# The first 60 microseconds by quarters of the channels instead of halves, in a two-block transformer kernel

## The reference

```python
mod = silu(cond) @ w + b                    # ada_w: 1024 x 6144, for the latent and the context condition
shift, scale, gate, ... = split(mod, 6)     # six parts of 1024 channels each
h = x * (1 + scale) + shift                 # on all 512 tokens (latent and context)
z = h @ conv_w_in                           # 1024 x 2560, five parts of 512 columns
a_val, a_gate, b_gate, c_gate, b_val = split(z)
ya = a_val * sigmoid(a_gate)                # then a depthwise convolution of 31 taps, a layer norm ...
```

## Time and profile before

| | |
|---|---|
| median of three runs | 1993.77 us (1989.11 to 1994.6) |
| span of the profiled execution | 1993.6 us |
| TensorE busy | 1775.0 us, 89% |
| VectorE busy | 1016.0 us, 51% |
| ScalarE busy | 418.9 us, 21% |
| GpSimd busy | 559.6 us, 28% |
| bytes moved | 574.31 MB, mean 288 GB/s |
| mean granted clock of TensorE | 0.953 |

### The profile page before, as it was taken

The page is one execution under the profiler, slowest core; times in us unless marked ns, Lnnn a source line. Parts: engine busy times, 40 slices in busy tenths (PEclk is TensorE's granted clock), DMA queues, the critical chain, the costliest instruction groups (busy, mean ns, idle before and its releaser), DMA issues.

```text
span 1993.6 us, 56691 instructions
## 1 busy us (share of the span) xinstructions
PE 1775.0 (89%) x23868; PEld 1227.3 (62%) x23869; DVE 1016.0 (51%) x2422; ACT 418.9 (21%) x838; POOL 559.6 (28%) x423
## 2 busy tenths in 40 slices
PE   7999989999999997999989966666669989999998
PEld 4544456656666664645766744444447767788887
DVE  3798156666676677247255633333347985110001
ACT  2001242211111214115342211111113224110001
POOL 0000026766766772001034523222257000100000
PEclk9999989999999998999989988888889899999999
DMA  9854177999999999514289999999996264433320
GB/s 364 323 207 169 42 264 324 429 428 429 410 430 411 430 428 392 194 46 158 85 330 417 430 429 428 429 428 428 429 409 218 102 234 171 169 127 127 129 104 21
DMA packets 109379, 574.31 MB, mean 288 GB/s; under 512 B 4977, under 2 KB 10225, under 8 KB 84593
## 3 DMA queue, kind: packets, MB, share of 16 engines
q1 hardware_dynamic: 108720, 570.72, 71.3%
q10 hardware_dynamic: 576, 2.43, 0.3%
HBM read 572.08 MB, written 1.05 MB: 287 GB/s over the span
## 4 chain that ended last, share of the span: by engine, by line
PE 64%; DMA 25%; DVE 7%; issue 2%; ACT 2%; SPq 1%; DVEq 0%; ACTq 0%
PE bank L355 25%; DMA ring<-in_expert_w_up 16%; PE bank L569 14%; DMA ring<-in_expert_w_down 8%; PE bank L541 4%; PE bank L999 4%; PE bank L519 3%; PE bank L616 3%; DVE b L1059 2%; PE bank L426 1%; ACT b L1879 1%; PE bank L915 1%; DVE b L1685 1%; DVE h_t L1059 1%; PE bank L718 1%
## 5 line engine op out<-in xcount | busy, mean ns | idle before, releaser
L569 PE MATMUL bank<-ring,b 128*32 128x128 f32 (+1 forms) x13600 | 517.8, 309 | 129.2 <-DMA ring<-in_expert_w_gate 67.1
L569 PEld LDWEIGHTS bank<-ring,b 128*32 128x32 f32 x13600 | 398.9, 115 | 302.5 <-issue 152.6
L1059 DVE TENSOR_TENSOR h_t<-h_t,bank 128x512 f32<-128x512 f32 (+1 forms) x696 | 349.5, 563 | 307.8 <-PE bank L541 307.8
L355 PE MATMUL bank<-h_t,ring 128*128 128x256 f32 (+1 forms) x1600 | 427.0, 429 | 5.9 <-ACT h_t L1879 5.9
L1879 ACT ACTIVATE b<-bank 128x256 f32<-128x256 f32 (+4 forms) x371 | 142.1, 400 | 1267.4 <-PE bank L569 742.3
L355 PEld LDWEIGHTS bank<-h_t,ring 128*128 128x128 f32 x1600 | 308.9, 194 | 117.6 <-issue 78.7
L2308 POOL TENSOR_SCALAR b<-b 128x1024 f32<-128x1024 f32 (+1 forms) x85 | 195.1, 2295 | 58.3 <-POOL b L2316 33.6
L2316 POOL TENSOR_TENSOR b<-b 128x512 f32<-128x512 f32 (+1 forms) x85 | 88.8, 1045 | 404.7 <-PE bank L541 404.7
L541 PE MATMUL bank<-b 32*128 32x512 f32 (+1 forms) x1392 | 171.0, 562 | 8.2 <-DVE h_t L1059 4.7
L1059 DVE TENSOR_TENSOR b<-b,bank 128x128 f32<-128x128 f32 (+3 forms) x124 | 49.9, 406 | 233.4 <-PE bank L355 155.1
L2311 POOL TENSOR_TENSOR b<-b,b 128x1024 f32<-128x1024 f32 (+1 forms) x85 | 161.4, 1899 | 7.1
(11 more groups left out here) (306 smaller groups left out, 1438.0 us busy)
## 6 DMA issues: line engine op xcount, KB each, us to landing
ring<-in_expert_w_gate SPq DMA_DIRECT2D x64, 2048.0 KB, 18.4
ring<-in_expert_w_up SPq DMA_DIRECT2D x64, 2048.0 KB, 20.7
ring<-in_expert_w_down SPq DMA_DIRECT2D x64, 2048.0 KB, 20.9
ring<-in_ada_w SPq DMA_DIRECT2D x24, 2048.0 KB, 14.1
ring<-in_w_mod SPq DMA_DIRECT2D x12, 2048.0 KB, 11.3
ring<-in_w_in SPq DMA_DIRECT2D x6, 2048.0 KB, 10.8
ring<-in_w_ffn_gate SPq DMA_DIRECT2D x5, 2048.0 KB, 8.5
ring<-in_w_ffn_up SPq DMA_DIRECT2D x5, 2048.0 KB, 7.7
```

Source lines behind the costliest of these rows:

```text
L355: last = pe.matmul(o, lhs(k), rhs(k), start=(k == 0), stop=(k == nk - 1))
L569: last = pe.matmul(b[32 * m:32 * m + 32, 0:width], lhs[:, k, :], rhs[:, k, m * width:(m + 1) * width], start=(k == 0), stop=(k == nk - 1), ...
L1059: return dv.tensor_tensor(o, a, b, op)
```

## The change

The halves become quarters of 256 channels (q = 0 to 3, k = 2q and 2q + 1).

- Chunks 0, 1, 3 and 4 hold a quarter each: 256 columns of shift and 256 columns of scale, loaded by two transfers of 1 MB whose rows in DRAM are 1 KB long. The tokens of a quarter come in two transfers of 256 KB, with rows of 1 KB. Conv0 is loaded in four parts of 512 KB, with rows of 2 KB as before. The order is tokens, shift, scale, conv0 part, four times over: 20 transfers of the same 12.6 MB instead of 15.
- On TensorE: turn tokens 0, piece 0, its turn; then for q = 0, 1, 2 the output groups m = 0 to 3 of the conv0 quarter q, with piece q + 1 behind m = 1 and its turn behind m = 2. The tokens of quarter 1 are turned behind m = 1 of quarter 0 and ahead of piece 1, those of quarters 2 and 3 behind m = 3 of quarters 0 and 1. Conv0's quarter 3 follows as the high half did. `turn_tokens(1)` and `(2)` wait for the tokens, the shift and the conv0 part of their quarter on one semaphore (64), `(3)` for tokens and shift (48).
- ScalarE takes all eight token tiles, two of them behind each modulation, and one copy per quarter takes shift and scale together. VectorE takes none. Each adds its part of a quarter's modulation. The two transfers of ScalarE still stand behind the last modulation.

```diff
-    before = [pieces[0], pieces[2], conv[0], pieces[1], pieces[3]] + pieces[EARLY:EARLY + 2]
+    quarters = [[rows(w["ada_w"][0], at + 256 * q, at + 256 * q + 256) for at in (0, D)] for q in range(EARLY)]
+    before = quarters[:2] + [conv[0]] + quarters[2:] + pieces[EARLY:EARLY + 2]
...
-            turn_tokens(range(4))
+            def turn_tokens(q):
+                pe.wait_ge(sem(f"quarter{q}" if q else "x_in"), (32, 64, 64, 48)[q])
+                for k in (2 * q, 2 * q + 1):
+                    group("a", lambda b: transposes(b, [(P * t, tok_in[:, t, k * P:(k + 1) * P]) for t in range(4)]))
+
+            turn_tokens(0)
...
-            early_pieces(0, 2)
-            mark("mods_low")
-            pe.wait_ge(sem("x_high"), 64)
-            turn_tokens(range(4, KD))
...
-            early_pieces(1, 3)
-            mark("mods")
+            early_piece(0)
+            early_turn(0)
+            conv0, first = chunk(conv_chunk(0), KD, 512), lane["v"]
+            for q in range(3):
+                if q == 0:
+                    pe.wait_ge(sem("conv_in"), 16)
+                for m in range(4):
+                    if q == 0 and first + m > 3:
+                        pe.wait_ge(v_free, first + m - 3)
+                    conv_quarter(V_BANKS[(first + m) % 4], q, m)
+                    if m == 1:
+                        if q == 0:
+                            turn_tokens(1)
+                        early_piece(q + 1)
+                    if m == 2:
+                        early_turn(q + 1)
+                if q < 2:
+                    turn_tokens(q + 2)
...
-            take_tokens((0, 2))
-            for half, event in enumerate(("mods_low", "mods")):
-                dv.wait_ge(a_free, marks[event][1])
+            for q in range(EARLY):
+                dv.wait_ge(a_free, marks[f"mods{q}"][1])
...
-                modulate(0, 0, "h_v0", ks=range(4 * half, 4 * half + 4))
-                if half == 0:
-                    take_tokens((4, 6))
+                modulate(0, 0, "h_v0", ks=(2 * q, 2 * q + 1))
...
+            for q, ahead in enumerate(((2, 3), (4, 5), (6, 7), ())):
+                take_piece(q)
+                take_quarter(q)
+                ac.wait_ge(sem("mods_ready"), q + 1)
                 ac.wait_ge(a_free, taken.n)
-                modulate(0, 0, "h_a0", ks=range(4 * half, 4 * half + 4))
-                if half == 0:
-                    take_tokens((5, 7))
+                modulate(0, 0, "h_a0", ks=(2 * q, 2 * q + 1))
+                take_tokens(ahead)
...
-            load(0, before[0])
-            load(1, before[1])
-            load_tokens(slice(512, D), "x_high")
-            sp.dma_start(chunk(2, KD, 512)[:, 0:4, :], before[2][:, 0:4, :]).then_inc(sem("conv_low"), 16)
-            load(3, before[3])
-            load(4, before[4])
-            sp.dma_start(chunk(2, KD, 512)[:, 4:KD, :], before[2][:, 4:KD, :]).then_inc(slot_loaded[2], 16)
+            for q in range(EARLY):
+                load_tokens(q)
+                n = piece_chunk(q)
+                shift, scale = before[n]
+                sp.dma_start(chunk(n, KD, 512)[:, :, 0:256], shift).then_inc(sem(f"quarter{q}"), 16)
+                sp.dma_start(chunk(n, KD, 512)[:, :, 256:512], scale).then_inc(slot_loaded[n], 16)
+                ks = slice(2 * q, 2 * q + 2)
+                sp.dma_start(chunk(2, KD, 512)[:, ks, :], before[2][:, ks, :]) \
+                    .then_inc((sem("conv_in"), sem("quarter1"), sem("quarter2"), slot_loaded[2])[q], 16)
```

More of the change, by code:

```diff
@@ L206, in piece_chunk @@
             if p < EARLY:
-                return (0, 3, 1, 4)[p]
+                return (0, 1, 3, 4)[p]
             if p < 12:
@@ L596, in _ @@
             pe.wait_ge(sem("params"), 32)
-            pe.wait_ge(sem("x_in"), 64)
             pe.wait_ge(sem("ones"), 5)
-            def turn_tokens(ks):
-                for k in ks:
-                    group("va"[k % 2], lambda b: transposes(b, [(P * t, tok_in[:, t, k * P:(k + 1) * P]) for t in range(4)]))
-            turn_tokens(range(4))
+            def turn_tokens(q):
[3 more added lines that the diff above has]
+            turn_tokens(0)
             pe.wait_ge(sem("cond_padded"), 2)
@@ L635, in piece_step, with early_piece, early_turn, conv_quarter @@
                     turn_piece(p - 1)
[L637 to L641, removed]
-            early_pieces(0, 2)
-            mark("mods_low")
-            pe.wait_ge(sem("x_high"), 64)
-            turn_tokens(range(4, KD))
[L647 to L652, removed]
+            def early_piece(q):
+                pe.wait_ge(sem(f"quarter{q}"), (16, 64, 64, 48)[q])
+                piece(q)
+            def early_turn(q):
+                turn_piece(q)
+                mark(f"mods{q}")
+            def conv_quarter(b, q, m):
+                for k in (2 * q, 2 * q + 1):
                     if m == 0:
@@ L655, in _ @@
                         pe.wait_ge(sem("h_a0"), k + 1)
-                    pe.matmul(V_BANKS[(first + m) % 4][:, :], wt[:, k, m * P:(m + 1) * P], H[:, k, :],
-                              start=(k == 0), stop=False)
-            early_pieces(1, 3)
-            mark("mods")
[L662 to L667, removed]
-                return last
+                    last = pe.matmul(b[:, :], conv0[:, k, m * P:(m + 1) * P], H[:, k, :], start=(k == 0), stop=(k == KD - 1))
+                return last
+            early_piece(0)
[16 more added lines that the diff above has]
+                    turn_tokens(q + 2)
             def early_sum(i):
@@ L694, in _ @@
                     else:
-                        group(which, lambda b: high_half(b, wt, m))
+                        group(which, lambda b: conv_quarter(b, 3, m))
                     mark(f"conv{j}_{m}")
@@ L1323, in _ @@
             done()
[L1324 to L1327, removed]
-            take_tokens((0, 2))
-            for half, event in enumerate(("mods_low", "mods")):
-                dv.wait_ge(a_free, marks[event][1])
-                for part in range(2):
[L1333 to L1336, removed]
+            for q in range(EARLY):
+                dv.wait_ge(a_free, marks[f"mods{q}"][1])
+                for part in range(2):
+                    at = 8 * part + 2 * q
+                    m = MOD[0][:, at:at + 2, :]
+                    step(dv.scalar_tensor_tensor(m, m, float(part), pr("ada_b0", at, 2).unsqueeze(2).broadcast_to([P, 2, 2]),
+                                                 ALU.add, ALU.add))
+                done()
                 dv.tensor_copy(st[:, 0:1], mods[:, 0:1]).then_inc(sem("mods_ready"), 1)
-                dv.wait_ge(sem("mods_ready"), half + 1)
-                modulate(0, 0, "h_v0", ks=range(4 * half, 4 * half + 4))
-                if half == 0:
-                    take_tokens((4, 6))
+                dv.wait_ge(sem("mods_ready"), q + 1)
+                modulate(0, 0, "h_v0", ks=(2 * q, 2 * q + 1))
             def early_sum(i):
@@ L2030, in take_tokens, with take_quarter @@
                     taken(act(X[:, k, :], b[:, :], ACT.Copy))
-            take_tokens((1, 3))
+            take_tokens((0, 1))
+            def take_quarter(q):
+                b = full()
+                both = MOD[0][:, 0:16, :].rearrange("p (s k) c -> p s k c", s=2)[:, :, 2 * q:2 * q + 2, :]
+                taken(act(both, v4(b, 0, 2, 2, 32)[:, :, :, 0:2], ACT.Copy))
             def take_turned(p):
@@ L2081, in _ @@
                     .then_inc(sem("conv_ya"), 1)
-            ac.wait_ge(sem("mods_ready"), 3)
+            ac.wait_ge(sem("mods_ready"), EARLY + 1)
             fetch_root()
@@ L2355, in _, with load_tokens @@
             c_rows = w["ctx"][0].rearrange("(t p) d -> p t d", p=P)
[L2356 to L2361, removed]
+            def load_tokens(q):
+                cols = slice(256 * q, 256 * q + 256)
+                event = sem(f"quarter{q}" if q else "x_in")
+                sp.dma_start(tok_in[:, 0:2, cols], x_rows[:, :, cols]).then_inc(event, 16)
+                sp.dma_start(tok_in[:, 2:4, cols], c_rows[:, :, cols]).then_inc(event, 16)
             def load(n, src):
```

## The result

The changed kernel takes 1997.62 us in the median of its 12 runs against 1990.7 us in the 12 of the kernel before beside it, 6.9 us more. The ratio on record is not the quotient of these two medians: it is 1.0024, with a 95% interval of 1.0012 to 1.0035, which is 4.8 us (2.4 to 7.0). The kernel has become slower, by about a quarter of a per cent. A second set gave 1.0017 (1.0005 to 1.0029). The profiled execution has a span of 1999.7 us against 1993.6; it is the second slowest of those that count. (One of the 12 executions took 2962.5 us at a mean granted clock of 0.555 and is left out of the ratio; without it the median is 1997.21 us.)

A forecast was written before the change was run, and what follows sets the result against it. Transfers up to conv1's landing were taken to run just level with TensorE. Counted as a shift of the first early sum, only the constants' term remained: 1993.77 + 1.0 = 1994.8 us, range 1989.5 to 1999.5, chance 0.58.

The forecast's parts named there:

- the constants' term: Ahead of conv1's first early sum: constants land at 65.7 us, bank free at 68.9 against 67.71; +1.2, taken as +1.0 us.
- conv1's landing: Conv1's weights land at 59 to 60.4 us, no later than conv0's end at 60.7, so this sets nothing.
- its own signs of being right: Included some 3 us of pause before the third token turn, and first early sum at 67 to 70 behind a VectorE wait.
- Rows of 1 KB: Early shift, scale and token transfers: 2.80 us per MB instead of 2.58, so 2.3 us more on 10.49 MB.
- Rival A: Early transfers: rows of 1 KB cost nothing and no clock is lost; -2.1 us, 1991.7; chance 0.18.
- Landings: Early transfers: quarters 1, 2 and 3 land at 22.2, 32.3 and 41.1 us, with 0.57 us per quarter for short rows.
- TensorE: Conv0 starts near 17 us, waits 3.2 us for quarter 2, and ends at 59.0 before any clock loss.
- Clock at 29 us: The pause ahead of quarter 2 brings the lower clock, 1.7 us lost (bounds 0 and 3.3); conv0 ends at 60.7.
- Rival C: ScalarE's constants land later than 12.4 us behind their issue; at 68.5 us, +4 us, 1997.8; chance 0.07.
- Rival B: Lower clock stays during conv0 from quarter 2 on; past +6 us, two whole quarters about +9, 2003; chance 0.12.
- Rival D: The change brings what it seems made for, conv1 and its bank 6 us earlier; about 1986 us; chance 0.05.

The follow-up runs named there:

- the two experiments on it: The kernel before with rows of 1 KB, and the changed kernel with rows of 2 KB; one run each, first early sum at 69.10 and 70.46 us.
- the remedies: Changed kernel with conv1's weights loaded ahead of piece 5 (ratio 0.9997), or constants first and parameters behind conv1's landing (0.9996); both together 0.9999.
- the three edits: Changed kernel with conv1 ahead of piece 5, parameters behind conv1's landing, and each quarter's tokens turned behind m = 1 of the quarter before; 1987.76 us, ratio 0.9976.
- added products: Products on data at hand, results overwritten, in TensorE's pauses: changed kernel ahead of conv1, 1.0028 and 1.0025; kernel with the three edits, ahead of 18 us, 0.9998.

## Why the prediction was right or wrong

The sign and the range held: 1994.8 us was forecast, 1997.62 measured, and +1.0 us against +4.8 by the ratio. (The 1993.77 us it started from were the median of three runs; twelve gave 1990.7.) The sign was right for another reason than the one given, and that is luck. The forecast's +1.0 us is the constants' term alone, which set nothing here; the loss came from conv1's landing, which the prediction had put at nothing. Three of its own signs of being right stayed out: the pause ahead of the third turn was 0.32 us and not some 3, the early sum stood at 72.72 and not between 67 and 70, and TensorE did not wait for VectorE ahead of it. Part by part:

- *Rows of 1 KB*: right, a little too dear. 2.80 us per MB (357 GB/s) was taken from a few us of another transfer; 347 to 367 GB/s stood in the windows, and 357 and 383 in the two experiments on it. Conv1's landing moved by 1.6 and 1.7 us for 8.39 MB, 0.19 to 0.20 us per MB where 0.22 was taken. The rule that 512 B are enough for full rate ("DMA: Bandwidth & Descriptors", section "Specifications", of the Trainium skill) does not hold here. The rows of 1 KB gave 357 GB/s over 30 us against 388 with rows of 2 KB, 8% less. The estimate of 4% from the packet overhead ("DMA: Bandwidth & Descriptors", section "Why small descriptors are slow (HBM only)", of the Trainium skill) is half of that. Rival A is out with it.
- *Landings*: right within 0.9 us. Quarter 2 at 31.4 (32.3 forecast), quarter 3 at 40.3 (41.1). *TensorE*: right. Conv0 from 17.9 (17), 26.9 us from the landing of quarter 2 to its end (26.7).
- *Clock at 29 us*: wrong in this execution. The groups ahead had already been slow (6.74 us instead of 3.67), so the pause was 0.32 us and not 3.2, nothing was lost behind it, and conv0 ended at 58.4 instead of 60.7. In other executions of the same start it came as forecast twice, 1.7 us each behind pauses of 2.59 and 1.92 us, and stayed out four times, behind pauses of 1.56, 1.91, 2.35 and 3.11 us: the length of the pause alone does not tell.
- *Conv1's landing*: this step failed. I let ScalarE's transfers "share the last 3 us" and had conv1 there at 59 to 60.4, hence "it sets nothing". They were issued at 50.56, and all of their 2.3 MB passed ahead of conv1: from quarter 3's 40.3 us, 6.3 + 2.3 MB at 388 GB/s give 62.5, and 62.7 was measured. The same sum on the kernel before (38.8 us, 8.6 MB) gives 61.0, against 60.3. The prediction's own numbers said as much: from 52.9 to 57.3 are 4.4 us and not 3, and at equal shares of the traffic (the parameters passed at about half of it, 1708 KB in 9.5 us) conv1 lands at 61.7, behind conv0's 60.7. Its second paragraph had also said that all of this traffic counts.
- *What was late next*: so the pause stood ahead of conv1, 4.36 us instead of none, with 3.1 us at the lower clock behind it. 62.78 - 60.84 = 1.9 us and 9.93 - 6.87 = 3.1 us are the 5.0 us. Both mechanisms stood in the prediction; the clock's was placed at 29 us.
- *The constants*: the mechanism was right, but not the bound here (bank free near 65.4, asked for at 72.7). With conv1 out of the way it became the bound, at 65.48, as the sum of 3.2 us said. Rival C is out for the changed kernel.
- *Slips in the sums, without effect on the outcome*: 1.2 us less the 0.5 to 1 named would be 0.2 to 0.7 and not 1.0; 22.2 + 6.5 is 28.7 and not 29.1; the kernel before has 14 early transfers on SyncE's queue and not 15, so six were added and not five.
- *Rival B*, a lower clock over most of conv0: not seen in any profile. *Rival D* came near its condition (conv1 and its bank 6 us earlier; 5.4 us were reached) only by the remedies and another place of the turns.

## What to carry to other kernels

When a beginning is cut finer so that compute can start earlier, first add up the bytes of every queue up to the next stage that needs data: compute that ends earlier than those land only waits, and may restart at the lower clock (here 4.36 us of waiting and 3.1 us more behind it). Finer cuts along the contiguous direction make rows shorter and shift that landing themselves. Look for what stands in the queue ahead of its need (here parameters and piece 5), and put no wait for the next part ahead of work whose data are there: the three edits together turned 1.0024 into 0.9976. Read the gain from repeated times and not from one profile: with added products the profiles of the first 70 us promised 2.5 to 4.0 us more than the runs gave.

## What the runs showed of the hardware that was not expected

While most rows are of 1 KB, windows of 3 us show 347 to 367 GB/s (357 over 30 us); with rows of 2 KB they show 383 over 30 us (the tokens still short) and up to 388, in the same place of the same kernel. Transfers issued on a second queue do not wait for the first one's backlog: 563 KB issued at 50.92 us, when conv1's 2 MB had been issued 14 us earlier, landed at 62.2, before conv1. And a stretch at 1.2 GHz moves from one execution of one kernel to the next (the same two groups took 6.74, 5.37 and, in other versions that are the same up to there, 3.67 us). A pause of 3.11 us was followed by full clock and one of 1.92 us by 3.4 us at 0.50, so a pause must be priced in more than one profile.
